# A decoder step whose conditioning blocks move from the sample attention to the retention's tiles

## The reference

```python
# layer, cut
u = modulate(layer_norm(x), shift, scale)       # shift, scale, gate = silu(c) @ w_ada
z = u @ w_in + b_in                             # q, k, v of four mixers, and 4 x 1024 gates
h_a = mlstm(...)                                # matrix memory, state C, n, m
h_b = latent_attention(...)                     # samples read 8 cache pages each
h_c = silu(layer_norm(causal_conv31(glu) + b))  # and the last 30 columns as new state
h_d = retention(...)                            # state S
y = sum(sigmoid(gates[n]) * (h[n] @ w_branch[n]) for n in range(4)) @ w_out
x = layer_norm(alpha * x + gate1 * y) * g + b
h = modulate(x, shift2, scale2)
x = layer_norm(alpha * x + gate2 * swiglu(h)) * g + b
```

## Time and profile before

| | |
|---|---|
| median of 3 runs | 1916.39 us |
| the profiled execution, its span | 1919.91 us, 1918.3 us |
| mean granted clock of TensorE, share of full speed | 0.941 |
| PE busy | 1730.8 us (90%) |
| DVE, ACT, POOL busy | 808.7, 739.9, 685.5 us |

### The profile page before, as it was taken

The page is one execution under the profiler, slowest core; times in us unless marked ns, Lnnn a source line. Parts: engine busy times, 40 slices in busy tenths (PEclk is TensorE's granted clock), DMA queues, the critical chain, the costliest instruction groups (busy, mean ns, idle before and its releaser), DMA issues. The chain is left out here.

```text
span 1918.3 us, 30351 instructions
## 1 busy us (share of the span) xinstructions
PE 1730.8 (90%) x10994; PEld 1487.5 (78%) x10994; DVE 808.7 (42%) x1909; ACT 739.9 (39%) x1122; POOL 685.5 (36%) x418
## 2 busy tenths in 40 slices
PE   3899999998799979999839999999997999799997
PEld 1788889885378859999717888898764778599996
DVE  0454465366531362332324535743565313623323
ACT  1456434333334244443224564342233341544422
POOL 0434546554022313332113445464530232133321
PEclk8899999998899989999968999999998999899999
DMA  9242365256764354444072523662667643544440
GB/s 359 78 183 101 99 105 198 89 176 227 295 229 166 127 198 146 143 152 154 23 284 88 184 98 89 109 215 91 213 222 262 240 151 123 207 147 142 152 154 28
DMA packets 81184, 309.12 MB, mean 161 GB/s; under 512 B 23746, under 2 KB 33282, under 8 KB 50946
## 3 DMA queue, kind: packets, MB, share of 16 engines
q1 hardware_dynamic: 81026, 307.09, 46.4%
HBM read 291.81 MB, written 15.25 MB: 160 GB/s over the span
## 5 line engine op out<-in xcount | busy, mean ns | idle before, releaser
L1981 POOL TENSOR_TENSOR wlx<-ring,wh 128x1024 fp32r<-128x1024 f32 x172 | 408.6, 2376 | 752.9 <-ACT wh L1031 748.1
L431 PE MATMUL zps<-uhi,wh 128*128 128x320 f32 x1232 | 385.4, 325 | 0.1
L432 PE MATMUL zps<-ulo,wh 128*128 128x320 f32 x1232 | 372.7, 314 | 0.0
L1031 ACT ACTIVATE wh<-ring 128x1024 fp32r<-128x1024 f32 x172 | 182.3, 1060 | 384.6 <-PE zps L432 255.6
L2073 POOL TENSOR_TENSOR wlo<-ring,whi 128x1024 fp32r<-128x1024 f32 x66 | 161.8, 2451 | 371.1 <-ACT whi L1031 371.1
L431 PEld LDWEIGHTS zps<-uhi,wh 128*128 128x128 f32 x1232 | 238.6, 194 | 12.7 <-issue 7.5
L432 PEld LDWEIGHTS zps<-ulo,wh 128*128 128x128 f32 x1232 | 239.0, 194 | 0.8
L890 PE MATMUL zps<-xhi,whi 128*128 128x320 f32 x704 | 221.3, 314 | 3.0 <-DVE xlo L1943 3.0
L891 PE MATMUL zps<-xlo,whi 128*128 128x320 f32 x704 | 220.2, 313 | 0.0
L892 PE MATMUL zps<-xhi,wlo 128*128 128x320 f32 x704 | 220.0, 313 | 0.0
L436 PE MATMUL zps<-uhi,wlx 128*128 128x320 f32 x1248 | 211.1, 312 | 0.0
(11 more groups left out here) (266 smaller groups left out, 2528.4 us busy)
## 6 DMA issues: line engine op xcount, KB each, us to landing
ring<-wpack_dram SPq DMA_DIRECT2D x222, 1024.0 KB, 4.9
arena<-cache_dram SPq DMA_DIRECT2D x128, 320.0 KB, 4.8
arena<-stateA_dram SPq DMA_DIRECT2D x2, 2064.0 KB, 9.6
o_cn_s<-arena SPq DMA_DIRECT2D x2, 2064.0 KB, 11.0
arena<-stateD_dram SPq DMA_DIRECT2D x2, 2048.0 KB, 11.9
o_ret_s<-arena SPq DMA_DIRECT2D x2, 2048.0 KB, 11.7
x<-o_y SPq DMA_DIRECT2D x2, 1280.0 KB, 7.5
o_y<-x SPq DMA_DIRECT2D x4, 640.0 KB, 3.0
```

The source lines that it names most:

```text
L431: nc.tensor.matmul(o, hi[:, k * P:(k + 1) * P], xh[:, k, :], start=k == 0, stop=False)
L432: last = nc.tensor.matmul(o, hi[:, k * P:(k + 1) * P], xl[:, k, :], start=False, stop=False)
L1031: return nc.scalar.activation(out, in_, func, **kw).then_inc(*ev(sem, label))
L1981: G().tensor_tensor(wlx[:, n % RING, half], ring[:, n % RING, half], wh[:, i, :], ALU.subtract).then_inc(*ev("pool_l", (q, i)))
```

## The change

- The conditioning blocks 8 to 15 follow the eight blocks of the retention's tiles, one each; 16 to 19 follow the four gate blocks of branch 0; 20 to 23 stand after the first feed-forward block. `weights()` looks a block up by its name.
- The attention has nine slots of exactly one dense block each (before: 10 dense blocks and 10 conditioning blocks in nine slots); gate block (1,6) comes after `sample_out`. `CONV_NORM` is 1 in place of 3.
- The samples' convolution state goes out from a compact copy `tail` that POOL makes, one block later in SP's order. `load_pages(0)` waits only for the prompt's retention state to be written.
- DVE does `weigh("a", 2)` and `decay(3)` ahead of `head_rows("a", 0)`; the 124 prompt taps are spread over the retention and the gate stages.
- At the entry of the feed-forward part: scale and shift are folded into the norm's gain and bias on small tiles, ACT makes the high half of the input straight from the normalised value, POOL makes the full one, and PE does the first tile in three sweeps (`first_tile`). The plain layer output is restored on DVE during the feed-forward part.

```diff
-          + [("in", f"{x}{i}", f"{x}{i + 1}") for x in ("dk", "dq", "dv", "dg") for i in (0, 2)])
+_ada = 8
+for _x in ("dk", "dq", "dv", "dg"):
+    for _i in (0, 2):
+        BLOCKS += [("in", f"{_x}{_i}", f"{_x}{_i + 1}"), ("ada", _ada)]
+        _ada += 1
...
+        for _i in (_h, _h + 2):
+            BLOCKS += [("in", f"g{_n}_{_i}", f"g{_n}_{_i + 1}")]
+            if _n == GATE_ORDER[0]:
+                BLOCKS += [("ada", _ada)]
...
-SLOTS = [[("gate", 2, 0)],
-         [("ada", 8), ("gate", 2, 2), ("ada", 9)],
-         [("ada", 10), ("ada", 11), ("ada", 12)],
-         [("ada", 13), ("ada", 14), ("ada", 15)],
-         [("branch", 2, 0), ("gate", 2, 4), ("ada", 16)],
-         [("gate", 2, 6), ("branch", 2, 4), ("ada", 17)],
-         [("gate", 1, 0), ("gate", 1, 2)],
-         [("gate", 1, 4)],
-         [("gate", 1, 6)]]
-CONV_NORM = 3
+SLOTS = [("gate", 2, 0), ("gate", 2, 2), ("branch", 2, 0), ("gate", 2, 4), ("gate", 2, 6), ("branch", 2, 4), ("gate", 1, 0), ("gate", 1, 2), ("gate", 1, 4)]
+CONV_NORM = 1
...
-BLOCKS += [("out", i) for i in range(4)] + [("ada", a) for a in range(18, 24)]
+BLOCKS += [("out", i) for i in range(4)] + FFN[:1] + [("ada", a) for a in range(20, 24)] + FFN[1:]
...
-                            sp.dma_start(of(dram("o_conv_s"), "p j b t"), ucs[:, :, :, TS:TS + CW - 1]).then_inc(C.sem("out_conv"), 16)
+                            sp.dma_start(of(dram("o_conv_s"), "p j b t"), tail).then_inc(C.sem("out_conv"), 16)
...
-                    head_rows("a", 0, W)
                     weigh("a", 2)
                     decay(3)
+                    head_rows("a", 0, W)
...
+                    def first_tile(o, hi, lo, name):
+                        for k in range(KC):
+                            pe.wait_ge(*at("act_x", ("samples", k // 4)))
+                            nc.tensor.matmul(o, hi[:, k * P:(k + 1) * P], xhi[:, k, :], start=k == 0, stop=False)
+                        pe.wait_ge(*at("pool_w", "first"))
+                        for k in range(KC):
+                            nc.tensor.matmul(o, lo[:, k * P:(k + 1) * P], xhi[:, k, :], start=False, stop=False)
+                        for k in range(KC):
+                            pe.wait_ge(*at("dve_x", k))
+                            last = nc.tensor.matmul(o, hi[:, k * P:(k + 1) * P], xlo[:, k, :], start=False, stop=k == KC - 1)
```

More of the change, by code:

```diff
@@ L448, in in_tiles, with turn @@
                                 fill[j]()
-                    def ada(a0, a1, through=True):
[L452 to L458, removed]
+                    def turn(p):
+                        turned[0] = 2 * p + 2
+                        pe.wait_ge(*at("act_mod", 2 * p + 1))
+                        ps = bank("m", ("adaT", p), ("dve_mod", ("sum", p)))
+                        for j in range(4):
+                            last = nc.tensor.transpose(ps[:, j * P:(j + 1) * P], rowb[:, j // 2, j % 2 * P:(j % 2 + 1) * P], ident)
+                        last.then_inc(*ev("pe_m", ("adaT", p)))
+                    def ada(a0, a1, through=True):
                         for i in range(a0, a1):
@@ L721, in slot, with conv_variance @@
                     def slot(b):
[L722 to L728, removed]
+                        kind, *which = SLOTS[b]
+                        if b == CONV_NORM:
+                            gate(*which, conv_variance, None)
+                        elif kind == "gate":
+                            gate(*which)
+                        else:
+                            branch(*which)
+                    def conv_variance():
+                        channel_sum("conv var", sqc, 4, ("act_cy", ("sq", 3)), ("act_cy", "std"))
                     def sample_scores(b):
@@ L1296, in slot @@
                     def slot(b):
-                        for kind, *which in SLOTS[b]:
-                            if kind == "gate":
-                                gates(*which, count=2, follow=which[0] == 1)
-                            elif kind == "branch" and which == [2, 0]:
-                                high(SPLIT.index(("in", "g2_4", "g2_5")))
-                            elif kind == "ada":
-                                nxt = BLOCKS[BLOCKS.index((kind, which[0])) + 1]
-                                if nxt in SPLIT:
-                                    high(SPLIT.index(nxt))
-                                ada(which[0], which[0] + 1)
+                        kind, *which = SLOTS[b]
+                        if b == CONV_NORM:
+                            gates(*which, count=1)
+                            conv_deviation()
+                            gates(which[0], which[1] + 1, count=1)
+                            conv_silu()
+                        elif kind == "gate":
+                            gates(*which, count=2)
                     for b in range(NB):
@@ L1733, in _, with taps @@
                     dve.wait_ge(*at("pe_m", ("ps", BH - 1, 1)))
-                    def taps(first, last):
-                        for i in range(first, last):
+                    tapped = [0]
+                    def taps(count):
+                        first, tapped[0] = tapped[0], min(tapped[0] + count, 4 * CW)
+                        for i in range(first, tapped[0]):
                             j, k = 2 * (i // (2 * CW)) + i % 2, i % (2 * CW) // 2
@@ L1863, in slot @@
                     def slot(b):
[L1864 to L1868 removed]
+                        kind, *which = SLOTS[b]
+                        if kind == "branch":
+                            gated(*which)
                     for b in range(NB):
```

297 lines of the change are left out of this document (177 added, 120 removed).

## The result

| | median of runs, us | ratio to the kernel before, 95% |
|---|---|---|
| before | 1915.82 (1905.80 to 1920.68, 20 runs) | |
| after | 1921.72 (1913.78 to 1933.78, 20 runs) | 1.0040 [1.0024, 1.0056] |

The change makes the kernel slower by 0.4%. The forecast was 1901 with a range up to 1919: wrong in sign, and just outside the range. The profiled execution took 1930.31 us, 8.6 above its kernel's median; that of the kernel before stood 4.1 above its own.

The account below looks back on a forecast made before the run. PE, busy 90% of the span, was taken to set the time with its work and gaps. The terms +15.0 − 20.2 − 1 + 9.4 − 10.7 gave −7.5 us a layer, −15 in all: 1901 us, range 1878 to 1919.

Parts of the forecast that it names:

- Work that is only moved: Twelve conditioning blocks and five turns come to the retention's tiles and branch 0's gates: +15.0 us a layer.
- Gates of branches 0 and 3: Later-issued loads make PE wait for a bank ScalarE's sigmoid frees: +9.4 us a layer, bounds 1 and 14.
- Retention's tiles: In retention, old gaps and low clock go, −11.7 us, new waits add 10.8: −1 a layer, bounds −9 and +4.
- Attention: Sample attention: conditioning blocks, old waits and low clock leave, new page waits add 7.7 us: −20.2 a layer.
- Entry: Feed-forward entry: second tile starts after 22.4 us, before 33.1: −10.7 a layer, bounds −12.5 and −6.
- by that rule −8: Feed-forward entry's gain if VectorE's low halves and GpSimd's eight full products exclude each other: −8 us a layer.
- the turn of the sign: Forecast's sign is wrong if retention and gates together grow by more than 31 us a layer.
- Rival 2: Ring bounds retention and gates: twelve "in" blocks, loaded one block ahead, each wait 2.7 us; 1925 us, chance 0.12.

Follow-up runs that it names:

- best2: Changed kernel with ScalarE making what PE awaits ahead of late blocks, GpSimd's wait as in lock, VectorE's head_rows first: 1868.76 us, ratio 0.9756; second run 1863.31.
- before_evict: Kernel before with only ScalarE's order changed: deviations and keys ahead of dq2's copy, both sigmoids ahead of both high halves before branch blocks: 1886.91 us, ratio 0.9836.
- evict_gates: Changed kernel with ScalarE's order turned round in branch 0's gates: sigmoid and token copies before the next block's high half: 1912.85 us, ratio 0.9988.
- noload: Changed kernel with conditioning blocks 8 to 19 neither loaded nor placed in the ring, their matmuls reading constants: 1888.01 us, ratio 0.9872.
- lock: Changed kernel with GpSimd starting the low half of feed-forward block 1 only after VectorE's eight low halves of the input: 1917.21 us, ratio 1.0014.
- convs: Changed kernel with the samples' convolution state written as before, from 4096 pieces of 30 numbers, at the new place: 1932.19 us, ratio 1.0104.

## Why the prediction was wrong

The mechanism was foreseen and came where it was named; no single step turned the sign. Four terms were each mis-sized by some 3 us a layer, all to the same side. At the forecast's own cuts, retention's tiles and then the gates up to g3_0's tile, layer 2 of the kernel after is this (before 88.2 and 66.5 us; in layer 1, 101.2 and 84.0 against 91.3 and 66.5):

```profile
1183.50:1284.66 101.16, 92.15 (x674) 81.03 (x673) 67.87 (x179) 33.06 (x46) 43.97 (x30) 0.93 0.49 170
1284.66:1368.33 83.67, 74.56 (x512) 61.89 (x513) 44.73 (x125) 25.10 (x37) 43.16 (x39) 0.96 0.47 172
```

| us a layer, moved work included | forecast | layer 1 | layer 2 | too good by, mean |
|---|---|---|---|---|
| retention's tiles (9.8 moved, −1) | +8.8 | +9.9 | +13.0 | 2.7 |
| gates and branch 0 (5.2 moved, +9.4) | +14.6 | +17.5 | +17.2 | 2.8 |
| attention | −20.2 | −19.2 | −14.2 | 3.5 |
| branch 1 to `ffn2`, with the entry | −10.7 | −7.9 | −6.4 | 3.6 |

- **Work that is only moved, +15.0: right.** 13.0 + 2.6 in best2 against before_evict.
- **Gates of branches 0 and 3, +9.4: a wait put at nothing.** The waits at the branches were right in place and nearly in size, 4.85 and 2.0 for 4.4 and 1.4, and so was the low clock, 2.6 and 2.9 for 2.5. But the turn behind block 16 (the expectation of evict_gates calls it 17) waited 3.0 and 2.3 us, with a copy of `tokens` stuck behind a late block, where I had nothing but 1.1 at a tile of g0_4 that did not wait. The term measured +12.3 and +12.0.
- **Retention's tiles, −1: inside its bounds, +0.1 and +3.2.** The waits of layer 2 were 9.0 us for my 7.6: 3.87 at `sample_a(2)` for 2.7, 2.6 for DVE's order as forecast, and 1.1 and 1.5 at two more places. The loads I had put at 6.8 us took 7.8 beside the small outputs and up to 9.8 beside the 2 MB ones (`o_cn_s` 13.2, `stateD` 13.3). And the low clock that I let go, 4.8 with 3.2 put back, did not go: in the first stretch PE's busy time rose by 10.9 and 13.7 for 12.4 of work, so on average 0.1 was saved.
- **Attention, −20.2: near in one layer, 6 too good in the other.** The long page waits came before batches 4, 5 and 7, as forecast (7.5 in all in layer 2, 9.1 in layer 1; I had 7.7), and the 2.7 at the norm stayed. What was mis-sized is the clock behind the waits: I took 2.4 us, and it was 2.0 and 8.2.
- **Entry, −10.7: a pass that waits for GpSimd, and a late block.** It gave −7.9 and −6.4; without the collision, and with the squares ahead of the copy of block 21, best2's stretch is 11.0 under before. I had the rule of the port in hand and priced it for GpSimd's eight products. Those did no harm; the pass that blocked was GpSimd's 2.36 us half of block 1, which follows them. The rule of the Trainium skill (page "SBUF — State Buffer", section "Who interferes with whom"), that the two exclude each other for a whole instruction, fits: the VectorE pass that began beside it took 2.70 us and not 0.49. The prediction's "by that rule −8" was nearer than my −10.7, but by luck, as it was priced for other passes. Another 0.95 us a layer went where PE waited for the squares, which stood on ScalarE behind the copy of block 21; its load was late by 0.86 and 1.18.

The prediction put the turn of the sign at 31 us a layer of growth in retention and gates. With the tiles around them they grew by 27.7 and 30.4 where I had 23.4, and the sign turned all the same, because the other two terms gave 7 us a layer less than forecast. Rival 2, with 1925 us near the measured time, had the cause (the load's lead is one dense block) and the sign, but not the mechanism: PE never waited for `wh` in the twelve blocks. ScalarE waited, 88 us of it in layer 2, and PE paid only where a result that it needed stood behind. That its number is near is luck.

Open: what decides whether the clock falls behind a page wait. In the same execution the eight cache products took 1.94 us behind the longest of these waits and 3.68 behind a shorter one:

```profile
560.17 1.94 PE L750 MATMUL mps<-arena,qabs 128*64 128x512 f32 x8 [3.02 <-DMA arena<-cache_dram]
...
1514.87 3.68 PE L750 MATMUL mps<-arena,qabs 128*64 128x512 f32 x8 [2.53 <-DMA arena<-cache_dram]
```

Nor does it belong to a layer. The eleven profiled kernels that have this attention with whole pages took 150.8 to 163.1 us for it, now in layer 1 (noload 163.0 and 153.9), now in layer 2 (the kernel after 153.7 and 158.2), on average 157 where I had 152.2. So the term was too low by some 5 us, and the difference between the two layers here is within the scatter.

## What to carry to other kernels

When a small block enters a ring of few slots it takes a slot as large ones do, and in this kernel's ring of three the next large load starts later by a whole block. Look then not at the engine that multiplies but at the one that prepares: in an in-order engine, let every wait for a load come after what others wait for. And look at the kernel before with the same eye: that order was worth 31 us there, more than the change ever promised.

## What the runs showed of the hardware

A wait on PE cost more than itself in this kernel: 4.5 us removed at branch (3,4) gave back 7.1 and 7.0 in the two layers, and a 2.2 us delay of one pass cost 4.8 and 3.7. Not each wait does: behind one of 3.02 us for pages the products ran at their usual 1.94 us. A VectorE pass of 0.49 us over two SBUF inputs that met a GpSimd pass of 2.36 us was held for all of it and took 2.70; when GpSimd waited 4.8 us for its turn instead (lock), no wait of PE for it appeared.

Beside a store of 480 KB in 4096 small pieces, which took 17.8 us, a 1 MB load took 15.3 us (convs); with the same bytes in 128 rows the store took 8.1 and the load beside it 7.8 (the kernel after).
